# A two-layer hybrid decoder with eight experts: expert results written to DRAM and fetched back per token, in place of scatter products

## The chip, the cores and the metric

The kernel runs on one core of one Trainium2 chip. The metric is the device time of one execution in microseconds (us), the median of several runs. TensorE is called PE, VectorE DVE, ScalarE ACT, GpSimd POOL and SyncE SP.

## The reference

The input x is 256 tokens of 1024 float32. Layer 0 is a state-space mixer beside block attention, then a dense SwiGLU; layer 1 is a linear recurrence beside sparse attention, then a mixture of experts; a final RMSNorm follows. The change touches only how the results of the experts come back to the tokens:

```
logits = xt @ router                      # 256 tokens x 8 experts
top_val, top_exp = top_k(logits, 2)       # two experts per token
gates = softmax(top_val)
...
for each expert e, for its tokens:        # xb: the token rows of e
    yb = (silu(xb @ w_gate[e]) * (xb @ w_up[e])) @ w_down[e]    # 1024 -> 3584 -> 1024
y[token] += yb * gate                     # two contributions per token
h = h + y
out = rms_norm(h, final_norm)
```

## The kernel before

Every engine has a program of its own, written out in order, and they meet at named semaphores. The experts are worked off as *items*. An item is up to 96 tokens (`CAP`) of one expert; items 0 to 7 are the first 96 tokens of experts 0 to 7, and further items exist only when an expert has more than 96 tokens. `n_items` is read from `work_list`, which the routing on DVE fills.

An item has 21 *blocks* (`NEB`), each a weight tile of 2 MiB: 7 of gate, 7 of up, 7 of down. The hidden width 3584 goes in four chunks c = 0 to 3 (`LAST` is 3, and is half as wide); the order is gate and up of c, then down of c-1. SP loads the blocks into seven ring slots: load j is issued once block j-7 has been used (`block_used`). PE multiplies a block in 48 float32 products at lines 2368 and 2370 (each shows as two in the trace, so 96); the hidden units stay token-major, so DVE multiplies (L1648) and turns them by 32x32 transposes (L1629), and ACT does the silu (L961). The item's result, 96 tokens x 1024, gathers in PSUM banks 4 and 5 over all the down blocks.

How a result comes back to its tokens, `it` being the item that follows it:
- ACT (`y_main`, L941 to L944) and DVE (`y_side`, L1606) copy banks 4 and 5 to the tile Y; DVE splits Y into a rounded part and the rest, Yhi and Ylo (L1612, L1614).
- PE multiplies by a 0/1 matrix that places each slot at its token (`scatter`, L2356 and L2357, four products of 512 columns for each half of the tokens), the first half after the second gate block of item `it`, the second half after its first up block.
- DVE adds the placed rows, times their gate, to `htok` (`add_scattered`, L1594).
- That 0/1 matrix is `mine`, made by DVE in chunk 1 of each item, turned (`turn_mine`, L1621), and copied by ACT (L967).

The tokens of the next items are gathered by products as well (`gather`, L2347, 32 products), after the up block of the last chunk of items 0, 2, 4 (for two items at once), 6 and 7. After the last item the same scatter and addition stand at the end, then the final norm and the store. POOL does nothing in this part.

## Time and profile before

| | us |
|---|---|
| median of 3 runs | 1593.23 |
| lowest and highest | 1591.78, 1594.74 |
| time of the profiled execution | 1591.04 |
| its span, first to last instruction | 1589.1 |
| PE busy | 1491.6 |
| DVE busy | 648.5 |
| ACT busy | 277.2 |
| POOL busy | 19.0 |

The span is what the profile covers; 1.94 us of the profiled execution's time lie around it. The experts' part runs from about 657 us to the end. "Busy" of an engine counts its own instructions; whether its time matters is told by who waits for it.

### The profile page before, as it was taken

What the parts mean: (1) busy time and instruction counts of PE and PEld (TensorE: products, weight loads), DVE (VectorE), ACT (ScalarE), POOL (GpSimd) and SP (SyncE); (2) the same over time, 40 slices, a digit from 0 to 9 for tenths busy, and PEclk for the clock granted to TensorE, in tenths of its full rate; (3) what the DMA queues carried; (4) which work ended last, traced back from release to release, by engine and by line L of the source; (5) the groups of instructions that cost most, each with busy time, mean ns of one, the idle gap of its engine ahead of it and who ended that gap; (6) DMA issues with size and microseconds to landing.
All of it is one profiled execution on the core that took longest, in us unless ns stands there. A gap on an engine that the chain in (4) does not pass through costs nothing.

```text
span 1589.1 us, 46789 instructions
## 1 busy us (share of the span) xinstructions
PE 1491.6 (94%) x21833; PEld 1418.5 (89%) x21833; DVE 648.5 (41%) x1486; ACT 277.2 (17%) x472; POOL 19.0 (1%) x21
## 2 busy tenths in 40 slices
PE   7898999997946889899999999999999999999997
PEld 6667999997934778899999999999999999999996
DVE  6933554447477641342142222322333223323323
ACT  3324443434234201200100000000001000001001
POOL 0000000000000210000000000000000000000000
PEclk9999999999966999799999999999999999999998
DMA  9131554463400008399999999999999999999980
GB/s 317 40 131 54 212 212 169 151 223 116 159 1 0 3 15 319 113 390 401 366 370 405 392 385 383 371 394 405 379 394 383 363 399 406 376 401 382 363 333 29
DMA packets 135653, 425.24 MB, mean 268 GB/s; under 512 B 9786, under 2 KB 12964, under 8 KB 135332
## 3 DMA queue, kind: packets, MB, share of 16 engines
q1 hardware_dynamic: 133536, 420.59, 69.6%
q8 instruction: 173, 2.83, 0.7%
q10 hardware_dynamic: 1924, 1.64, 0.4%
q14 instruction: 20, 0.16, 0.0%
HBM read 421.18 MB, written 1.05 MB: 266 GB/s over the span
## 4 chain that ended last, share of the span: by engine, by line
PE 87%; DVE 10%; ACT 2%; issue 1%; DMA 0%; SPq 0%; DVEq 0%; ACTq 0%
PE bank L2370 36%; PE bank L2368 19%; PE bank L1992 5%; PE bank L1994 5%; PE bank L1993 5%; PE bank L1967 2%; PE bank L1736 1%; PE bank L2347 1%; PE bank L1980 1%; PE bank L1902 1%; PE bank L1985 1%; DVE xnT L1008 1%; PE bank L2356 1%; PE bank L2200 1%; PE bank L2185 1%
## 5 line engine op out<-in xcount | busy, mean ns | idle before, releaser
L2370 PE MATMUL bank<-ring,yT 128*32 128x128 f32 x5760 | 635.5, 273 | 0.0
L2368 PE MATMUL bank<-ring,yT 128*32 128x384 f32 x5760 | 631.3, 489 | 1.1 <-ACT yT L934 1.1
L2370 PEld LDWEIGHTS bank<-ring,yT 128*32 128x32 f32 x5760 | 627.6, 110 | 0.0
L2370 PE MATMUL bank<-ring,arena 128*32 128x128 f32 x2304 | 255.6, 273 | 0.0
L2368 PE MATMUL bank<-ring,arena 128*32 128x384 f32 x2304 | 255.1, 490 | 0.0
L2370 PEld LDWEIGHTS bank<-ring,arena 128*32 128x32 f32 x2304 | 251.1, 110 | 0.0
L1994 PE MATMUL bank<-arena_r,ring_r 128*128 128x256 f32 x688 | 193.8, 282 | 0.0
L1629 DVE STREAM_TRANSPOSE arena<-arena 32x192 f32<-32x192 f32 x384 | 142.0, 370 | 124.5 <-PE bank L2370 119.4
L2368 PEld LDWEIGHTS bank<-ring,yT 128*32 128x32 f32 x5760 | 182.0, 108 | 6.4 <-issue 5.1
L1648 DVE TENSOR_TENSOR arena<-arena,bank 128x384 f32<-128x384 f32 x56 | 28.9, 551 | 310.4 <-PE bank L2370 285.9
L1992 PE MATMUL bank<-arena_r,ring_r 128*128 128x256 f32 x528 | 147.9, 280 | 1.3 <-DVE arena_r L1249 1.3
L1993 PE MATMUL bank<-arena_r,ring_r 128*128 128x256 f32 x528 | 147.2, 279 | 0.0
L961 ACT ACTIVATE arena<-bank 128x384 f32<-128x384 f32 x56 | 24.9, 489 | 694.7 <-PE bank L2370 694.7
L1236 DVE TENSOR_TENSOR ring_r<-ring,ring_r 128x2048 fp32r<-128x2048 f32 (+1 forms) x46 | 98.7, 2152 | 89.5 <-ACT ring_r L729 89.4
L1994 PEld LDWEIGHTS bank<-arena_r,ring_r 128*128 128x128 f32 x688 | 130.8, 190 | 0.0
L1992 PEld LDWEIGHTS bank<-arena_r,ring_r 128*128 128x128 f32 x528 | 99.2, 188 | 1.7 <-issue 1.4
L729 ACT ACTIVATE ring_r<-ring 128x2048 fp32r<-128x2048 f32 (+1 forms) x46 | 82.7, 1802 | 95.0 <-PE bank L1994 89.3
L1993 PEld LDWEIGHTS bank<-arena_r,ring_r 128*128 128x128 f32 x528 | 99.1, 188 | 0.1
L2368 PEld LDWEIGHTS bank<-ring,arena 128*32 128x32 f32 x2304 | 65.0, 108 | 0.4
L1594 DVE SCALAR_TENSOR_TENSOR arena<-bank,arena 128x512 f32<-128x512 f32 x32 | 22.5, 746 | 97.2 <-PE bank L2357 97.2
L1992 PE MATMUL bank<-yT_r,ring_r 128*128 128x256 f32 x160 | 46.8, 293 | 8.9 <-DVE arena_r L1242 5.5
L1736 PE MATMUL bank<-xnT,ring 128*128 128x256 f32 x192 | 45.6, 398 | 8.0 <-DVE arena L1206 5.7
(450 smaller groups left out, 1364.7 us busy)
## 6 DMA issues: line engine op xcount, KB each, us to landing
ring<-in_moe_w_gate SPq DMA_DIRECT2D x56, 2048.0 KB, 10.6
ring<-in_moe_w_up SPq DMA_DIRECT2D x56, 2048.0 KB, 10.7
ring<-in_moe_w_down SPq DMA_DIRECT2D x56, 2048.0 KB, 10.7
ring<-in_ffn_w_gate SPq DMA_DIRECT2D x5, 2048.0 KB, 8.1
ring<-in_ffn_w_up SPq DMA_DIRECT2D x5, 2048.0 KB, 7.8
ring<-in_ffn_w_down SPq DMA_DIRECT2D x5, 2048.0 KB, 7.8
ring<-in_o_w_in SPq DMA_DIRECT2D x5, 2048.0 KB, 7.9
ring<-in_e_w_in SPq DMA_DIRECT2D x4, 2048.0 KB, 16.6
```

The lines of the kernel that those rows point to most:

```text
L729: act_.activation(pair(h, src.shape[1])[0], src, ACT.Copy).then_inc(sem("hi_done"), 1)
L961: last = act_.activation(MO["silu"][:, FM * i:FM * i + FM], bank[i][:, 0:FM], ACT.Silu)
L1236: v.tensor_tensor(lo, src, hi.bitcast(f32), SUB).then_inc(sem("lo_done"), 1)
L1629: last = v.transpose(to[QUAD[b], :, 32 * a:32 * a + 32], Hc[QUAD[a], 0:to.shape[1], 32 * b:32 * b + 32])
L1648: last = v.tensor_tensor(MO["H"][:, s_], MO["silu"][:, s_], bank[2 + i][:, 0:FM], MUL)
L1736: last = pe_.matmul(dst(i)[0:width, :], w[:, k, i * P:i * P + width], xnT[:, k, :], start=(k == 0), stop=(k == KD - 1))
L1967: last = pe_.matmul(half(bank[2 + i // 2], i), view(n + i // 4)[:, k, (i % 4) * P:(i % 4) * P + P], yT[:, k, :], start=(k == 0), stop=(k = ...
L1992: pe_.matmul(dst, w[0], x[0], start=start, stop=False, skip_group_check=True)
L1993: pe_.matmul(dst, w[1], x[0], start=False, stop=False, skip_group_check=True)
L1994: return pe_.matmul(dst, w[0], x[1], start=False, stop=stop, skip_group_check=True)
L2368: pe_.matmul(b[QUAD[m], 0:FM], x(m), w[:, 0:FM], start=start, stop=stop, skip_group_check=True)
L2370: last = pe_.matmul(b[QUAD[3], P * m:P * m + P], x(m), w[:, FM:FB], start=start and m == 0, stop=stop, skip_group_check=True)
```

## The change

The results of items 0 to 6 are no longer placed by products. Each is copied to Y as before and then stored by ACT, as 96 rows of 1024 float32 (393,216 bytes), in a DRAM tensor `expert_rows` (`y_store`). In item 0 DVE works out for each token, from its rank in each expert, which two rows are its own (`find_rows`, 18 small operations). When the result of item 6 is stored, POOL issues four indirect transfers, each of 128 rows of 4 KB, into the space of `xnT` and `hT` (2 MiB in all), and in the last chunk of item 7 DVE adds the fetched rows, times their gates, to `htok` (`add_rows`, four operations of 128x1024). A result of expert 7, or of an item beyond 7, is still placed by the products. ACT and DVE write items 0 to 7 out; a loop for items from 8 on follows, which a branch skips if there are none. Before, item 7 was the loop's first turn. Semaphores that the left-out products would have raised are raised in advance.

```diff
+    rows_dram = nc.dram_tensor("expert_rows", ((NE - 1) * CAP, D), f32, kind="Internal").ap()
+    row_of = sb("row_of", NT * 2, i32)
+    rows_in = [flat(x)[:, i * D:i * D + D] for x in (xnT, hT) for i in range(2)]
+    def scattered_by_products(it):
+        return not isinstance(it, int) or it >= NE - 1
...
# POOL
+        pool.wait_ge(sem("mlo_rows_ready"), 2)
+        pool.wait_ge(sem("x_in_Y_out"), 16 * NE)
+        for j in range(NT * 2):
+            pl.indirect_dma_start(rows_in[j], None, rows_dram, bass.IndirectOffsetOnAxis(ap=row_of[:, j:j + 1], axis=0)
+                                  ).then_inc(sem("rows_loaded"), 16)
...
# ACT
+        def y_store(n):
+            act.wait_ge(sem("Y_copied"), 2 * n + 1)
+            act.wait_ge(sem("Y_side"), n)
+            act.dma_start(rows_dram[(n - 1) * CAP:n * CAP, :], MO["Y"][0:CAP, :]).then_inc(sem("x_in_Y_out"), 16)
         def y_main(n):
+            if not isinstance(n, int):
+                act.wait_ge(sem("x_in_Y_out"), 16 * NE)
+            elif n > 1:
+                act.wait_ge(sem("x_in_Y_out"), 16 * n)
...
-            act.wait_ge(sem("mineT_done"), it + 1)
-            act_.activation(mineT[0:CAP, :], mineT0[0:CAP, :], ACT.Copy).then_inc(sem("mineT_copied"), 1)
+            if scattered_by_products(it):
+                act.wait_ge(sem("mineT_done"), it + 1)
+                act_.activation(mineT[0:CAP, :], mineT0[0:CAP, :], ACT.Copy).then_inc(sem("mineT_copied"), 1)
...
-        for it in range(1, NE - 1):
+        for it in range(1, NE):
             run_item(it)
         n_items = act.value_load(work_list[0:1, ITEMS:ITEMS + 1], min_val=NE, max_val=ITEMS)
-        with act.Fori(NE - 1, n_items) as it:
-            run_item(it)
+        with act.If(n_items > NE):
+            with act.Fori(NE, n_items) as it:
+                run_item(it)
...
# DVE, whose loop over the items is changed in the same way
         def y_side(n):
...
             last.then_inc(sem("Y_side"), 1)
+            if isinstance(n, int):
+                return
...
+        def add_rows():
+            dve.wait_ge(sem("rows_loaded"), 16 * NT * 2)
+            for i in range(2):
+                for t in range(NT):
+                    last = v.scalar_tensor_tensor(htok[:, t, :], rows_in[2 * t + i], row_gate[:, t, i:i + 1],
+                                                  htok[:, t, :], MUL, ADD)
...
-            if not peeled:
+            if not isinstance(it, int):
                 for t in range(NT):
                     dve.wait_ge(sem("scatter_done"), NT * it + t + 1)
                     add_scattered(t, 6, sem("scattered"))
...
+                    if peeled:
+                        find_rows()
...
+                if kind == "gate" and c == LAST and isinstance(it, int) and it == NE - 1:
+                    add_rows()
...
# PE
+                if kind == "down" and c == 0 and x == 0 and not peeled:
+                    pe.wait_ge(sem("Y_copied"), 2 * it + 1)
+                    pe.wait_ge(sem("Y_side"), it)
...
-                if kind == "gate" and c == 0 and x == 1 and not peeled:
+                if kind == "gate" and c == 0 and x == 1 and not isinstance(it, int):
                     pe.wait_ge(sem("Yhi_ready"), 2 * it + 1)
                     pe.wait_ge(sem("Ylo_ready"), NT * it)
                     pe.wait_ge(sem("mineT_copied"), it)
                     pe.wait_ge(sem("scattered"), NT * it)
                     scatter(0)
-                if kind == "up" and c == 0 and x == 0 and not peeled:
+                if kind == "up" and c == 0 and x == 0 and not isinstance(it, int):
                     pe.wait_ge(sem("scattered"), NT * it + 1)
                     scatter(1)
```

On PE, at the end of the second gate block of item 1, before the change (`bank` is PSUM, `ring` a weight slot, `yT` the gathered tokens, `arena_r` the placing matrix and the split result):

```order
2988 L2368 MATMUL bank<-ring,yT 32x384 x3
2989 L2370 MATMUL bank<-ring,yT 32x128 x3
2990 L2356 MATMUL bank<-arena_r 128x512 [waits mineT_copied,scattered,Ylo_ready,Yhi_ready]
2991 L2357 MATMUL bank<-arena_r 128x512
2992 L2356 MATMUL bank<-arena_r 128x512
2993 L2357 MATMUL bank<-arena_r 128x512
2994 L2368 MATMUL bank<-ring,yT 32x384 [waits slot1_loaded,H_done]
```

After the change PE has at the same place of item 1:

```order
2986 L2444 MATMUL bank<-ring,yT 32x384 x3
2987 L2446 MATMUL bank<-ring,yT 32x128 x3
2988 L2444 MATMUL bank<-ring,yT 32x384 x3
2989 L2446 MATMUL bank<-ring,yT 32x128 x3
2990 L2444 MATMUL bank<-ring,yT 32x384 [waits slot1_loaded,H_done]
2991 L2444 MATMUL bank<-ring,yT 32x384 x2
```

The four products and the wait for four semaphores are gone, and the gate block is followed at once by the up block; the same holds after the first up block.

On DVE, at the start of item 1, before (L1606 copies a part of Y, L1594 adds the placed rows):

```order
594 L1606 COPY arena<-bank 32x128 [waits block_used]
595 L1606 COPY arena<-bank 32x128 x2
596 L1612 TENSOR_SCALAR arena_r<-arena 96x512 [waits Y_copied,Y_side]
597 L1614 TENSOR_TENSOR arena_r<-arena,arena_r 96x512 [waits Yhi_ready]
598 L1612 TENSOR_SCALAR arena_r<-arena 96x512 [waits Y_copied]
599 L1614 TENSOR_TENSOR arena_r<-arena,arena_r 96x512 [waits Yhi_ready]
600 L1594 SCALAR_TENSOR_TENSOR arena<-bank,arena 128x512 [waits scatter_done]
601 L1594 SCALAR_TENSOR_TENSOR arena<-bank,arena 128x512
602 L1594 SCALAR_TENSOR_TENSOR arena<-bank,arena 128x512 [waits scatter_done]
603 L1594 SCALAR_TENSOR_TENSOR arena<-bank,arena 128x512
604 L1648 TENSOR_TENSOR arena<-arena,bank 128x384 [waits HT_done,block_used,moe_silu]
```

And on DVE in the last chunk of item 7 after the change (`xnT` and `hT` hold the fetched rows):

```order
730 L1667 STREAM_TRANSPOSE arena<-arena 32x6x32 [waits H_done,block_used]
731 L1667 STREAM_TRANSPOSE arena<-arena 32x6x32 x15
732 L1698 SCALAR_TENSOR_TENSOR arena<-xnT,arena 128x1024 [waits rows_loaded]
733 L1698 SCALAR_TENSOR_TENSOR arena<-hT,arena 128x1024
734 L1698 SCALAR_TENSOR_TENSOR arena<-xnT,arena 128x1024 [waits dve_chain]
735 L1698 SCALAR_TENSOR_TENSOR arena<-hT,arena 128x1024
736 L1718 TENSOR_TENSOR arena<-arena,bank 128x384 [waits HT_done,block_used,moe_silu]
737 L1667 STREAM_TRANSPOSE yT<-arena 32x3x32 [waits H_done]
```

The eight operations from L1612 to L1594 leave the start of items 1 to 7, and the four additions stand once, ahead of the last multiplication of item 7.

On ACT, at the start of item 1 after the change:

```order
290 L965 ACTIVATE arena<-bank 96x384 [waits block_used]
291 L966 ACTIVATE arena<-bank 96x384
292 L968 ACTIVATE arena<-bank 32x128 x3
293 L956 DMA expert_rows<-arena 96x1024 [waits Y_side,Y_copied]
294 L987 ACTIVATE arena<-bank 128x384 [waits H_done,block_used]
```

The store is new there; the row after it, the silu, stood directly behind the copies before.

## Rows read from the trace of the kernel before

**Rows 1.** The page: span; PE's busy time; granted clock in 40 slices.
```profile
span 1589.1 us, 46789 instructions
PE 1491.6 (94%) x21833; PEld 1418.5 (89%) x21833; DVE 648.5 (41%) x1486; ACT 277.2 (17%) x472; POOL 19.0 (1%) x21
...
PEclk9999999999966999799999999999999999999998
```

**Rows 2.** Waits of PE from 620 us on: total, times, longest.
```profile
PE bank L2356 <- DVE arena_r L1614: 3.4, 1, 3.4
...
PE bank L2368 <- ACT yT L934: 1.1, 1, 1.1
```

**Rows 3.** Timeline of PE around a scatter in item 2: start, us, instruction.
```profile
893.29 0.82 PE L2370 MATMUL bank<-ring,yT 128*32 128x128 f32 x6
894.04 0.50 PE L2356 MATMUL bank<-arena_r 96*128 96x512 f32 x1
...
894.84 0.40 PE L2357 MATMUL bank<-arena_r 96*128 96x512 f32 x1
895.16 0.52 PE L2368 MATMUL bank<-ring,yT 128*32 128x384 f32 x3
```

**Rows 4.** Timeline of SP's issues of weight loads, without and across scatters.
```profile
662.41 0.37 SPq L497 DMA_DIRECT2D ring<-in_moe_w_up  x1
...
746.25 5.61 SPq L497 DMA_DIRECT2D ring<-in_moe_w_up  x2
...
781.58 7.02 SPq L497 DMA_DIRECT2D ring<-in_moe_w_down  x2
...
894.14 7.02 SPq L497 DMA_DIRECT2D ring<-in_moe_w_down  x2
```

**Rows 5.** Groups by line from 620 us on: the scatter's products.
```profile
L2356 PE MATMUL bank<-arena_r 96*128 96x512 f32 x32 | 15.1, 472 | 3.4 <-DVE arena_r L1614 3.4
```

**Rows 6.** Timeline of PE at the gather of item 2.
```profile
980.40 3.82 PE L2347 MATMUL bank<-arena_r 128*128 128x192 f32 x32
984.15 0.52 PE L2368 MATMUL bank<-ring,arena 128*32 128x384 f32 x3
```

**Rows 7.** Busy time by stretch; last three: granted clock, DMA share, GB/s.
```profile
669.00:782.00 113.00, 113.00 (x2026) 112.46 (x2018) 32.74 (x98) 6.26 (x17) 0.00 (x0) 1.00 1.00 388
...
1270.00:1350.00 80.00, 80.00 (x1473) 80.00 (x1465) 25.07 (x76) 3.35 (x9) 0.00 (x0) 1.00 1.03 402
```

**Rows 8.** Line 497: issue to landing at 662, from 678 to 756, from 660 to 1450.
```profile
DMA to landing us min/median/max: 7.7/7.7/7.7
...
DMA to landing us min/median/max: 10.2/10.9/11.2
...
DMA to landing us min/median/max: 7.6/10.7/12.0
```

**Rows 9.** Timeline of DVE in item 0, chunk 1: turning the hidden units.
```profile
709.58 6.12 DVE L1629 STREAM_TRANSPOSE arena<-arena 32x192 f32<-32x192 f32 x16 [5.19 <-PE bank L2370]
```

**Rows 10.** Groups of DVE at the routing, 630 to 656 us: one small operation.
```profile
L1525 DVE TENSOR_TENSOR arena<-arena 128x16 f32<-128x16 f32 x2 | 0.4, 176 | 0.1
```

**Rows 11.** Timeline of ACT after the copies of Y, item 2.
```profile
894.15 0.87 ACT L961 ACTIVATE arena<-bank 128x384 f32<-128x384 f32 x2 [8.77 <-PE bank L2370]
```

**Rows 12.** Timeline of DVE in the last chunk of item 7, to the end.
```profile
1544.46 6.12 DVE L1629 STREAM_TRANSPOSE arena<-arena 32x192 f32<-32x192 f32 x16 [9.46 <-PE bank L2370]
1554.94 0.55 DVE L1648 TENSOR_TENSOR arena<-arena,bank 128x384 f32<-128x384 f32 x1 [4.36 <-PE bank L2370]
...
1574.51 0.91 DVE L1606 COPY arena<-bank 32x128 f32<-32x128 f32 x3 [14.46 <-PE bank L2370]
```

**Rows 13.** Groups by line from 620 us on: an operation of 128x1024 on DVE.
```profile
L1681 DVE SCALAR_TENSOR_TENSOR arena<-arena 128x1024 f32<-128x1024 f32 x2 | 2.6, 1285 | 0.1
```

**Rows 14.** DMA issues: KB each, us to landing.
```profile
out_dram<-arena SPq DMA_DIRECT2D x2, 512.0 KB, 2.6
...
ring<-in_s_b_re SPq DMA_DIRECT2D x2, 64.0 KB, 5.2
```

More of the change, by code:

```diff
@@ L954, in run_item @@
                 y_main(it)
+                if isinstance(it, int):
+                    y_store(it)
             for j, (kind, c, x) in enumerate(expert_blocks):
@@ L1631, in turn_hidden, with find_rows @@
             last.then_inc(sem("HT_done"), 1)
+        row1, row_gate = (MO["cnt"][:, x:x + NT * 2].rearrange("p (t i) -> p t i", t=NT) for x in (0, NT * 2))
+        def find_rows():
+            wide = [P, NT, NE]
+            link(v.tensor_scalar(flat(e1), flat(rank), 0.0, None, ALU.is_ge))
+            link(v.scalar_tensor_tensor(flat(e1), flat(rank), float(CAP), flat(e1), ALU.is_lt, MUL))
+            link(v.memset(e1[:, :, NE - 1:NE].rearrange("p t o -> p (t o)"), 0.0))
+            link(v.tensor_scalar(e2[:, 0, :], C("expert"), float(CAP), 1.0, MUL, ADD))
+            link(v.tensor_tensor(t16, rank, e2[:, 0:1, :].to_broadcast(wide), ADD))
+            link(v.tensor_tensor(flat(t16), flat(t16), flat(e1), MUL))
+            link(v.tensor_reduce(row1[:, :, 0], t16, AX, ALU.max))
+            link(v.tensor_reduce(row1[:, :, 1], t16, AX, ADD))
+            link(v.tensor_tensor(row1[:, :, 1], row1[:, :, 1], row1[:, :, 0], SUB))
+            link(v.tensor_tensor(flat(e1), flat(e1), flat(gate), MUL))
+            for i in range(2):
+                link(v.tensor_tensor(e2, t16, row1[:, :, i:i + 1].to_broadcast(wide), ALU.is_equal))
+                link(v.tensor_tensor(flat(e2), flat(e2), flat(e1), MUL))
+                link(v.tensor_reduce(row_gate[:, :, i], e2, AX, ADD))
+            link(v.tensor_scalar(flat(row1), flat(row1), -1.0, 0.0, ADD, ALU.max))
+            v.tensor_copy(row_of[:, :], flat(row1)).then_inc(sem("mlo_rows_ready"), 1)
+        def add_rows():
+            dve.wait_ge(sem("rows_loaded"), 16 * NT * 2)
+            for i in range(2):
+                for t in range(NT):
+                    last = v.scalar_tensor_tensor(htok[:, t, :], rows_in[2 * t + i], row_gate[:, t, i:i + 1],
+                                                  htok[:, t, :], MUL, ADD)
+                if not i:
+                    link(last)
         def run_item(it, peeled=False):
@@ L1652, in run_item @@
                         onehots(it + 1, next_items(it))
-                    for t in range(NT):
-                        v.tensor_copy(MO["gnow"][:, t:t + 1], gatep[:, t, bass.ds(it, 1)])
-                    for t in range(NT):
-                        last = v.tensor_scalar(mine[:, t, :], C("time")[:, 0:CAP], slotp[:, t, bass.ds(it, 1)], None,
-                                               ALU.is_equal)
-                    last.then_inc(sem("mine_ready"), 1)
-                    dve.wait_ge(sem("mine_ready"), it + 1)
-                    turn_mine()
+                    if peeled:
+                        find_rows()
+                    if scattered_by_products(it):
+                        for t in range(NT):
+                            v.tensor_copy(MO["gnow"][:, t:t + 1], gatep[:, t, bass.ds(it, 1)])
+                        for t in range(NT):
+                            last = v.tensor_scalar(mine[:, t, :], C("time")[:, 0:CAP], slotp[:, t, bass.ds(it, 1)],
+                                                   None, ALU.is_equal)
+                        last.then_inc(sem("mine_ready"), 1)
+                        dve.wait_ge(sem("mine_ready"), it + 1)
+                        turn_mine()
+                if kind == "gate" and c == LAST and isinstance(it, int) and it == NE - 1:
+                    add_rows()
                 if kind == "up" and x == halves(c) - 1:
@@ L1667, in _ @@
         run_item(0, peeled=True)
-        for it in range(1, NE - 1):
+        for it in range(1, NE):
             run_item(it)
         n_items = dve.value_load(work_list[0:1, ITEMS:ITEMS + 1], min_val=NE, max_val=ITEMS)
-        with dve.Fori(NE - 1, n_items) as it:
-            run_item(it)
+        with dve.If(n_items > NE):
+            with dve.Fori(NE, n_items) as it:
+                run_item(it)
         y_side(n_items)
```

37 lines of the change are left out of this document (23 added, 14 removed).

## The prediction

> **What bounds the kernel now.** I read the page first. PE is busy in 1491.6 of 1589.1 us, and nearly all slices but those of the middle stand at the high clock [rows 1]. A busy PE could still be a slow one that is fed late, so the next view is its list of waits. From 620 us to the end PE waits at most 3.4 us in one place (L2356 at the very end, for Ylo) and 1.1 us in another [rows 2]. Through eight items it waits neither for a weight nor for DVE or ACT. PE's own instructions therefore set the time there, and an instruction taken from it shortens the kernel unless another engine cannot follow.
>
> PE's pace is best read from SP, which issues a load each time PE has used up a block. From 662.41 to 746.25 us there are 16 such steps without any scatter between them: 83.84 / 16 = 5.24 us for a block [rows 4]. From 781.58 to 894.14 us are the 21 steps of item 1 with its two scatters: 112.56 us [rows 4]. The granted clock was 1.00, the 2.4 GHz level, in the stretches read [rows 7]. Twenty-one blocks alone would be 110.04 us, so the two scatters cost 2.52 us in an item, 1.26 us each. The timeline of one agrees: its four products begin at 894.04 and the next block begins at 895.16 us, 1.12 us later [rows 3]; the remaining 0.14 us is PE draining and filling again on both sides.
>
> The other engine to watch is the DMA. Its share is 1.00 to 1.03 in the items, at 388 to 402 GB/s [rows 7], so it looks as full as PE. That share does not say which of them waits. The time to landing does: a lone load of 2 MiB lands after 7.7 us, loads in the steady stretch after 10.2 to 11.2 us, and none between 660 and 1450 us after more than 12.0 us [rows 8]. A load is issued when its slot is freed and is needed six blocks later, 6 x 5.24 = 31.4 us. So at the median of 10.7 us there are 20.7 us of slack.
>
> **The change part by part.**
>
> *Scatter products off PE.* L2356 has 32 instructions, four to an item, so exactly eight items run and none is of a second turn [rows 5]. The scatters of items 0 to 6, which stand inside items 1 to 7, go; that of item 7, at the end, stays. Seven items x 2.52 us = **17.6 us less**. All of it lies on the path, because PE had no idle time around them [rows 2, 3].
>
> *New waits on PE.* At its first down block of an item PE now waits for the copies to Y. These are made at the item's start, and the block is eight blocks or 42 us later, so it is passed at once. Queued behind it would be all of PE; price nothing.
>
> *Y stores on ACT.* ACT now waits for its own and DVE's copies and issues a transfer. What is queued behind is the silu, for which PE waits in turn; but ACT idles 8.77 us before it [rows 11], and an issue takes 0.37 us on SP's queue [rows 4]. The copies of the next item wait for a store made 110 us earlier. A store of 512 KB landed in 2.6 us on a free queue [rows 14], and some 12 us in the full one is the same bound as for a weight. Price nothing on ACT.
>
> *find_rows on DVE, item 0.* Eighteen operations of some 0.18 us [rows 10], with the wait after each about 3.8 us. They stand in chunk 1, where DVE idles 5.19 us before it may turn the hidden units [rows 9], and the operations on `mine` and their turning, which stood in the same gap, leave in that item. Nothing; without that cover 3.8 us once.
>
> *Work that leaves DVE.* Yhi, Ylo and the additions; DVE is not waited for. Nothing.
>
> *add_rows on DVE, item 7.* Four operations of 128x1024, nearest row 1.285 us [rows 13]: 5.1 us. DVE ends its transposes at 1544.46 + 6.12 = 1550.6 us and idles 4.36 us until the last up block is through [rows 12]. So the last product of silu and up comes some 0.9 us later. PE meanwhile gathers for 3.75 us [rows 6] and needs that product only for the last quarter, 2.8 us in; the product takes 0.55 us [rows 12], so 1.3 us are left. Nothing; without that cover 0.9 us.
>
> *The end.* ACT and DVE load n_items and branch over the new loop behind item 7 instead of leaving the old one. DVE idles 14.46 us there [rows 12]. Nothing. The last scatter, the addition and the norm are the same.
>
> *DMA.* This is the only follower that may fail. PE will ask for a block every 5.24 us, 2.097 MB / 5.24 = 400 GB/s, with only the gathers (3.75 us) to catch up in. Added are 0.393 MB for a store in each item (1.0 us of DMA time at 388 GB/s) and 2.1 MB of fetched rows at the start of item 7 (5.4 us). From above: the DMA kept 402 GB/s over 80 us [rows 7], and then nothing piles up but the additions, 7 x 1.0 + 5.4 = 12.4 us, less four gathers of 3.75 us. From below: it can do 388 GB/s and no more, the least of the rows. A block then takes 5.41 us; it falls behind by 3.5 us in an item, with the store 4.5; seven items make 31.5, less four gathers 15.0, plus the fetch 5.4: 21.9 us against 20.7 of slack, a wait of 1.2 us at the end. So the price is 0 to 1.2 us, and if the gathers gave nothing back, 16 us. I take 0: between 678 and 756 us, some 15 loads with one gather and no scatter among them, landings stayed within 10.2 to 11.2 us [rows 8], which is what a DMA that can follow looks like.
>
> The Trainium skill (HBM Reference, Specifications) speaks against the change: it gives a core some 358 GB/s as its share of the memory it has in common with its neighbour, and about 425 when it streams alone. By the first figure a block would take 5.86 us, the kernel would be bound by its loads before and after, and the change would lose the extra traffic; which is the first rival at its extreme; the trace's 402 GB/s disagrees. By the second a block takes 4.93 us and nothing piles up.
>
> *Sum.* 1591.04 - 17.6 = 1573.4 us for an execution like the profiled one. That one lies 2.2 us under the median of the runs shown, so the median should be 1593.23 - 17.6 = **1575.6 us**.
>
> **The rivals.**
> - *The DMA falls behind* and PE waits for weights in items 5 to 7. For it: a share of 1.00, and more bytes in less time. Against it: the slack of 20.7 us and rows 8. The time: 1577 (the wait of 1.2 us) to 1592 (no catching up at all), the middle 1581. Chance 0.11.
> - *The fetch comes late: slower.* The indirect transfers are the one kind that the trace doesn't have. If they went in small pieces as the 64 KB of s_b_re did, which took 5.2 us to land [rows 14], 2048 KB would take 32 x 5.2 = 166 us. They start once item 6's result is stored, near 1470 us in the old times, and DVE wants them at 1550.6: 80 us. They would be 86 us late; DVE stands, the last product is missing, PE stands: 1575.6 + 84 = 1660 us. It turns into a loss when the fetch takes over 80 + 1.3 + 17.6 = 99 us, 21 GB/s. Against it: a fetched row is 4 KB in one piece. Chance 0.04.
> - *A few us given back at the edges:* the start of POOL's first transfers, or the branch at the end. The Trainium skill (Runtime: NRT & Kernel Launch, Instruction fetch mechanics) says that a taken branch out of the two loaded pages has to fetch before it goes on. In rows: such a stall on DVE or ACT has 14.46 us of cover [rows 12], and one of over that would show as a longer wait of PE at the end; 1577 to 1580. Chance 0.07.
> - *Nothing is saved because the products still run:* only with an item beyond 7, which rows 5 rule out for these inputs. Chance 0.
>
> **How the numbers follow.** The forecast has chance 0.78, with a range of its own of 1573 to 1578 (the runs before spread by 3 us). Reaching into the first and third rival, the range 1571 to 1583 holds 0.88 or so by these chances, and I keep that reach, since the cost of the DMA is the least known. A measurement of this kernel tells some 0.2%, 3.2 us, from no change. Faster by more than that: the forecast, the edges and most of the DMA rival, 0.94. Within: the worst of the DMA rival, 0.02. Slower: 0.04.
>
> **What would show it.** In the changed kernel an odd item should last 110.0 us by SP's steps and a block still 5.24; PE's list of waits should stay near what it is. L2356's heir should have 4 instructions. Times to landing may climb to some 16 or 20 us; PE waiting on a weight slot, with landings above 31 us, would be the first rival. A gap of DVE before the four additions would be the second. The prediction is wrong if blocks themselves become slower than 5.24 us, which no row gives a reason for.

## The result, and the profile after

The changed kernel takes 1581.49 us, the median of 4 runs (1581.04 to 1585.56), beside 1593.8 us for the kernel before: a ratio of 0.993, interval 0.9917 to 0.9942. In a second set of runs it took 1579.07 us (5 runs) against 1593.91 us, ratio 0.991 (0.9897 to 0.9923). So it is faster by 12 to 15 us where 17.6 us were forecast. The execution that was profiled first is the slowest of its four, 1585.56 us, and what stands below of it shows more loss than a middle one has.

The page of the changed kernel, answering to [rows 1]:

```profile
span 1583.6 us, 46515 instructions
...
PE 1487.0 (94%) x21777; PEld 1419.3 (90%) x21777; DVE 598.6 (38%) x1340; ACT 275.0 (17%) x465; POOL 22.9 (1%) x25
...
PEclk9999999998975999699999999999999999999998
```

DVE has lost 50 us of work and PE only 4.6 us of busy time, though 56 products went and seven times 2.52 us should be gone. Two single executions don't settle that: PE was busy for 1499.1 us in the second profile of the kernel before (before_again, below) and for 1476.9 us in the second one of the changed kernel. Where time was given back has to be read stage by stage.

The group of the scatter's products by line, the heir of [rows 5], and the timeline of PE at two gathers (start, us, instruction):

```profile
L2432 PE MATMUL bank<-arena_r 96*128 96x512 f32 x4 | 2.6, 662 | 3.4 <-DVE arena_r L1652 3.4
```

```profile
759.87 3.82 PE L2423 MATMUL bank<-arena_r 128*128 128x192 f32 x32
...
983.83 3.81 PE L2423 MATMUL bank<-arena_r 128*128 128x192 f32 x32
```

Four products are left of 32. From gather to gather are two items: 983.83 - 759.87 = 223.96 us. SP's issues, answering to [rows 4], have 21 blocks in 900.09 - 790.05 = 110.04 us, where the kernel before took 112.56 us:

```profile
790.05 5.76 SPq L505 DMA_DIRECT2D ring<-in_moe_w_down  x2
...
900.09 5.76 SPq L505 DMA_DIRECT2D ring<-in_moe_w_down  x2
...
1463.57 7.75 SPq L505 DMA_DIRECT2D ring<-in_moe_w_down  x2
```

The saving of 2.52 us in an item is there to the last digit. The third row is the odd one: its two issues span 7.75 us instead of 5.6, so one block of item 7 took 2.1 us too long.

What PE waits for, from 620 us on (total, times, longest), answering to [rows 2]:

```profile
PE bank L2432 <- DVE arena_r L1652: 3.4, 1, 3.4
...
PE bank L2408 <- DVE arena_r L1619: 0.7, 1, 0.7
PE bank L2446 <- issue: 0.4, 1, 0.4
```

No weight is in the list. Two rows matter. The gather of item 0 (L2408) waits 0.7 us, where it waited 0.36 us; and there is an "issue" row, time in which PE waited for nothing that the profile shows. Time from issue to landing of the weight loads (L505) from 678 to 756, from 780 to 1450 and from 1450 us on, answering to [rows 8]:

```profile
DMA to landing us min/median/max: 9.2/11.0/11.8
...
DMA to landing us min/median/max: 8.6/12.1/15.1
...
DMA to landing us min/median/max: 11.5/15.4/17.8
```

The landings climb, to 17.8 us at most, and 31.4 us would be needed before PE stands. The new transfers by queue, from the page, and by issue (median us to landing), from the view of the DMA:

```profile
q0 software_dynamic: 576, 2.10, 0.3%
...
xnT<-expert_rows,row_of POOLq DMA_INDIRECT x2, 10.1
hT<-expert_rows,row_of POOLq DMA_INDIRECT x2, 12.9
```

The 2.1 MB of rows land 10 to 13 us after their issue near 1465 us, and the additions begin at 1545 us.

PE at the gather of item 0, up to the first block of the experts. First the kernel before, then the changed one:

```profile
651.76 4.02 PE L2332 MATMUL bank<-arena_r,arena 128*128 128x96 f32 x32 [0.36 <-DVE arena_r L1587]
...
656.93 0.52 PE L2368 MATMUL bank<-ring,yT 128*32 128x384 f32 x3 [1.15 <-ACT yT L934]
```

```profile
657.13 7.13 PE L2408 MATMUL bank<-arena_r,arena 128*128 128x96 f32 x32 [0.67 <-DVE arena_r L1619]
665.41 0.52 PE L2444 MATMUL bank<-ring,yT 128*32 128x384 f32 x3 [1.15 <-ACT yT L948]
```

The same 32 products take 7.13 us instead of 4.02 us, and the first block comes 8.28 us after the gather's start instead of 5.17 us. The wait comes from DVE, which is itself idle ahead of the one-hot tile, 0.25 us before the change and 0.54 us after it:

```profile
651.26 0.45 DVE L1587 TENSOR_SCALAR arena_r<-con,arena 128x96 fp32r<-128x96 f32 x2 [0.25 <-DVE arena L1578]
```

```profile
656.63 0.45 DVE L1619 TENSOR_SCALAR arena_r<-con,arena 128x96 fp32r<-128x96 f32 x2 [0.54 <-DVE arena L1607]
```

In the program two semaphore increments stand at this place before the change and five after it. Busy time by stretch shows why (the last three columns are granted clock, DMA share and GB/s); the changed kernel at the first gather, ahead of the gather of item 7, right behind it, and in POOL's burst:

```profile
657.00:665.00 8.00, 7.13 (x32) 6.90 (x32) 0.07 (x1) 0.64 (x3) 0.00 (x0) 0.55 0.00 0
1400.00:1430.00 30.00, 30.00 (x556) 30.00 (x552) 6.93 (x18) 1.36 (x3) 0.00 (x0) 1.00 1.03 405
1436.00:1442.00 6.00, 6.00 (x89) 5.58 (x85) 0.99 (x4) 0.57 (x3) 0.00 (x0) 0.75 0.85 335
1465.00:1469.00 4.00, 3.57 (x45) 1.82 (x44) 0.00 (x0) 0.00 (x0) 2.44 (x3) 1.00 1.03 418
```

Near 0.5 is the 1.2 GHz level: in the first stretch PE ran nearly all of the gather on it, where the kernel before had 0.90 over the same work:

```profile
651.00:657.00 6.00, 4.49 (x37) 3.93 (x40) 0.46 (x3) 1.12 (x5) 0.00 (x0) 0.90 0.00 0
```

In the third, behind the gather of item 7, it is at 0.75, so half of 6 us at the low level. In the fourth the clock is full, and PE's loads have done 44 instructions in 4 us, where a block has 96 of each kind in 5.24 us. Those are three losses, and each got experiments.

### The profile page after: what moved, and what is told of

The parts are those of the page before. It is cut to its first block, busy times and chain, and to the rows that moved or that the text cites. A ratio compares the mean times of both kernels' runs of the same rounds, so it can differ in the third digit from the quotient of the medians.

```text
span 1583.6 us, 46515 instructions
## 1 busy us (share of the span) xinstructions
PE 1487.0 (94%) x21777; PEld 1419.3 (90%) x21777; DVE 598.6 (38%) x1340; ACT 275.0 (17%) x465; POOL 22.9 (1%) x25
## 4 chain that ended last, share of the span: by engine, by line
PE 87%; DVE 9%; ACT 2%; issue 1%; DMA 0%; SPq 0%; DVEq 0%; ACTq 0%
PE bank L2446 37%; PE bank L2444 19%; PE bank L2068 5%; PE bank L2070 5%; PE bank L2069 5%; PE bank L1812 2%; PE bank L2043 2%; PE bank L2423 1%; PE bank L2056 1%; PE bank L1978 1%; PE bank L2061 1%; DVE xnT L1037 1%; PE bank L2276 1%; PE bank L2274 1%; PE bank L2261 0%
## 5 line engine op out<-in xcount | busy, mean ns | idle before, releaser
L2446 PEld LDWEIGHTS bank<-ring,yT 128*32 128x32 f32 x5760 | 628.5, 110 | 1.7 <-issue 1.7
L2444 PEld LDWEIGHTS bank<-ring,yT 128*32 128x32 f32 x5760 | 155.9, 108 | 1.9 <-ACT yT L948 1.4
L1812 PEld LDWEIGHTS bank<-xnT,ring 128*128 128x128 f32 x192 | 39.2, 207 | 15.3 <-DVE arena L1235 5.8
```

Source lines behind the costliest of these rows:

```text
L1812: last = pe_.matmul(dst(i)[0:width, :], w[:, k, i * P:i * P + width], xnT[:, k, :], start=(k == 0), stop=(k == KD - 1))
L2444: pe_.matmul(b[QUAD[m], 0:FM], x(m), w[:, 0:FM], start=start, stop=stop, skip_group_check=True)
L2446: last = pe_.matmul(b[QUAD[3], P * m:P * m + P], x(m), w[:, FM:FB], start=start and m == 0, stop=stop, skip_group_check=True)
```

## The experiments

The kernel before ran beside each of the three later sets of runs, at 1593.91, 1593.73 and 1594.07 us, 11 runs each time. The ratios are to these, and in the first row to 1593.8 us (4 runs).

| kernel | median us (runs) | ratio, interval | gather start to first block | behind item 7's gather | gap in POOL's burst |
|---|---|---|---|---|---|
| changed, first | 1581.49 (4) | 0.993, 0.9917-0.9942 | 8.28 | low clock | yes |
| changed_again | 1579.07 (5) | 0.991, 0.9897-0.9923 | 8.26 | low clock | no |
| no_fetch | 1578.5 (6) | 0.9913, 0.9897-0.9929 | 6.85 | full | none issued |
| direct_fetch | 1577.83 (4) | 0.9899, 0.9885-0.9913 | 4.96 | low clock | none issued |
| no_return_path | 1579.7 (5) | 0.9912, 0.99-0.9925 | 6.69 | full | none issued |
| wide_gather | 1580.85 (6) | 0.992, 0.9906-0.9934 | 6.82 | full | yes |
| late_fetch | 1582.26 (6) | 0.9929, 0.9916-0.9943 | 8.24 | low clock | yes |
| stores_x4 | 1580.57 (5) | 0.9917, 0.9903-0.9931 | 8.25 | low clock | yes |
| fetch_twice | 1580.75 (6) | 0.9924, 0.9908-0.9939 | 6.83 | full | no |
| direct_twice | 1579.97 (6) | 0.992, 0.9898-0.9941 | 8.26 | low clock | none issued |
| sems_later | 1577.52 (4) | 0.9899, 0.9884-0.9913 | 5.26 | low clock | no |
| combined | 1575.14 (4) | 0.9885, 0.9871-0.99 | 5.26 | full | no |

The last three columns are read from the one profiled execution of each, in the timeline of PE. The two profiles of the kernel before have 5.17 and 5.17 us, and full clock.

The columns hold a tie that no experiment was made for. All five profiles with 8.2 or 8.3 us ahead of the first block have the low clock behind item 7's gather. None of the four with 6.7 to 6.9 us has it, and three of these gather 96 columns there like the first five. Of the three with 5.0 to 5.3 us, the two narrow ones have it and the wide one hasn't. Between the first block and that gather PE takes the same 766.4 us in every one of the twelve. So whether the clock falls there seems to hang on when it rose at the start of the experts, and the first two losses aren't independent; why, no run here shows.

**The changed kernel and the kernel before, again.** No edit. One profile each can't tell a property of a kernel from one of an execution.

> The changed kernel once more, nothing edited. In its first profile the experts began at 665.4 us (656.9 before the change) and the last item lost 3.7 us: 2.0 us in a gap of PE inside a block while POOL issued the fetch, and some 1.9 us at the low clock right after the gather at 1431.8. Theory A: the 2.0 us belong to the fetch and come back at the same place; the low clock after the gather and the late start of the experts belong to the single execution. Then the experts' stretch (from the first block to the last scatter) is 905 us, the experts begin within 3 us of 657, and the time is 1578 to 1582. Theory B: both belong to the change (more bytes, a longer start): the experts begin some 8 us late again and the low clock is there again; the time is near 1585.

> The kernel before, once more, for its profile. Its first profile came from the fastest of its runs (1591.0 against a median of 1593.9 us) and its experts began at 656.9 us. In five profiles of the changed kernel and its variants they began at 660.0 to 665.4 us, and the low clock before them lasted longer. Theory A: the stretch ahead of the experts differs from execution to execution in both kernels, and the first profile was a lucky one: they begin at 659 to 665 us now. Theory B: the changed kernel itself loses 3 us and more there: they begin within 1 us of 656.9. In both the experts' stretch should be 920.9 us, unless the clock falls after a gather.

The profile of changed_again shows the late clock at the first gather and the low clock behind item 7's, but no gap in POOL's burst: PE stood in one execution and not in the other, with POOL's transfers at the same place in the program. before_again took 1596.52 us in its one run. Its experts' stretch, first block to last scatter, is 921.2 us beside 920.9 us in the first profile, but the gather of item 0 begins at 657.01 us, not 651.76 us:

```profile
657.01 4.02 PE L2332 MATMUL bank<-arena_r,arena 128*128 128x96 f32 x32 [0.39 <-DVE arena_r L1587]
```

So the stretch ahead of the experts, which the change doesn't touch but for its setting up, differs by 5 us between two executions of one kernel. At 650 us the first profile of the changed kernel was 5.1 us behind the first of the kernel before, and changed_again 0.3 us ahead of it. What differs between the kernels must be read inside the experts' stretch: 920.9 and 921.2 us before, 906.9 and 904.9 us after, where 17.6 us less would be 903.3.

**Without the fetch and the additions.** POOL issues nothing, DVE adds nothing; experts 0 to 6 are missing from the result.

```diff
-        for j in range(NT * 2):
-            pl.indirect_dma_start(rows_in[j], None, rows_dram, bass.IndirectOffsetOnAxis(ap=row_of[:, j:j + 1], axis=0)
-                                  ).then_inc(sem("rows_loaded"), 16)
...
-                    add_rows()
```

> The changed kernel without POOL's four indirect transfers and without the four additions of the fetched rows (the results of experts 0 to 6 are missing in the output); the stores stay. If the fetch makes PE's gap in the last item, the gap is gone and the time falls by 2.0 us against the changed kernel. If the gap comes from something else in the last item (the unrolled code of DVE and ACT, the waits on the stores), it stays and the time is that of the changed kernel within 0.5 us. Times to landing in the last item should not jump from 14 to 18 us.

Measured 1578.5 us beside 1579.07 us for changed_again on the same chip: no difference that can be measured. Item 7, from its first block to the next gather, takes 110.18 us, with no loss in it:

```profile
1430.92 0.52 PE L2437 MATMUL bank<-ring,arena 128*32 128x384 f32 x3
...
1541.10 3.77 PE L2416 MATMUL bank<-arena_r 128*128 128x96 f32 x32
```

The fetch and the additions together are therefore worth little at the median, and the missing 3 us or so must come from elsewhere too.

**The rows fetched by plain transfers on ACT's queue.** The same bytes at the same time, but in row order, so that DVE adds rows that aren't the token's own.

```diff
+                    if c == 0 and isinstance(it, int) and it == NE - 1:
+                        act.wait_ge(sem("x_in_Y_out"), 16 * NE)
+                        for r in range(NT * 2):
+                            act.dma_start(rows_in[r], rows_dram[P * r:P * r + P, :]).then_inc(sem("rows_loaded"), 16)
```

> The changed kernel with the 2 MiB read by four plain transfers from ACT's queue, 128 rows in order, in place of POOL's indirect ones (so the rows added to a token are not its own), issued after the first silu of item 7, at nearly the same time. If it is the bytes that take PE's instructions or weights away, PE has the same gap of about 2 us. If it is POOL's making of the descriptors, the gap is gone and the time is that of no_fetch, 2.0 us less than the changed kernel, while the times to landing jump as before.

1577.83 us. Its profile has no gap in item 7 and happens to have the shortest first gather of those that keep the setting up as it is (4.96 us), but the low clock behind item 7's gather. The bytes themselves cost nothing that shows.

**Without the whole return path.** No fetch, no stores of Y, no waits for them, no indices; experts 0 to 6 are missing.

```diff
-                if isinstance(it, int):
-                    y_store(it)
...
-                    if peeled:
-                        find_rows()
```

> The changed kernel without stores, without the search for rows, without fetch and additions (the results of experts 0 to 6 are missing in the output): only the products are gone. This is the value of the 56 scatter products alone. By the prediction it is 17.6 us under the kernel before. If the stores cost nothing, it equals no_fetch within 0.5 us; if they slow PE or the loads, it lies lower, at most 7 us. The longest time to landing should stay near 13 us instead of climbing to 15.

1579.7 us, no faster than the changed kernel. The stores, the waits that came with them and `find_rows` cost nothing that shows, as they were priced; and even with all of this added work gone 14 us are saved, not 17.6. The increments ahead of the first gather are still in this kernel. What is missing is in what the change does to PE's timing, not in the work that it adds.

**A gather of 192 columns behind item 6.** The changed kernel gathers 96 columns there, for item 7 alone; this one gathers for a pair, and half of it goes unused.

```diff
-            return 1
+            return 2
```

> The changed kernel with the gathers behind items 6 and 7 made for two items, as those behind items 0, 2 and 4 are: 192 columns in each of the 32 products in place of 96. In three of five profiles of variants the granted clock fell to 1.2 GHz right at the end of the gather behind item 6, which cost 1.9 us, and never after the wide ones. If the narrow products matter, the fall is gone, PE's time for the gather stays at 3.7 us, and item 7 takes 110.2 us; the median falls by up to 1.9 us. If the fall has to do with the place alone, it comes after this gather too.

The clock stays at its full level behind the gather, in this profile and in that of combined, which has the same edit. A stretch of combined, with the first block behind the gather starting at 1428.06 us in its middle:

```profile
1425.00:1431.00 6.00, 6.00 (x86) 5.90 (x87) 4.34 (x17) 1.64 (x4) 0.00 (x0) 1.00 1.03 410
```

But wide_gather's median is 1580.85 us; the fall by up to 1.9 us that was expected didn't come. Its profiled execution had the gap in POOL's burst, so its item 7 took 112.10 us. The low clock came in 7 of 10 profiles of changed variants with the narrow gather, in neither of the two with the wide one, and in neither of the kernel before, whose gather there is narrow as well. Two against three of ten is no proof, and wide_gather itself is one of the four profiles with 6.7 to 6.9 us, whose narrow ones had the full clock too. Only sems_later and combined, alike at 5.26 us, speak for the width, so that it matters stays open. What it costs is read: item 7 takes 111.84 us with it (changed_again, sems_later) and 110.18 us without, 1.7 us.

**The fetch late.** POOL also waits until item 7's last seven weight loads have landed, and the additions move behind the last turning of the hidden units.

```diff
+        for j in range(NEB - SLOTS, NEB):
+            pool.wait_ge(*expert_place(NE - 1, j)[1:])
```

> The changed kernel with the fetch issued only when the last weight blocks have landed, and the four additions behind the last turning of the hidden units in item 7, while PE works on the last down block. The fetch then shares the DMA with nothing. If the 2.0 us gap that PE had in item 7 in one of two profiles comes from the fetch beside the weight loads, it cannot come here, and times to landing in item 7 should not exceed 15 us. If the fetch takes over some 20 us, DVE's additions come late and the end moves: 1 to 5 us slower. Otherwise the time is that of the changed kernel or up to 1 us less.

The gap moved with the fetch. The timeline of POOL and that of PE's loads in this kernel:

```profile
1534.75 1.11 POOL L582 DMA_INDIRECT xnT<-expert_rows,row_of  x1 [951.10 <-DMA ring<-in_moe_w_down]
...
1538.65 0.93 POOL L582 DMA_INDIRECT hT<-expert_rows,row_of  x1 [0.30 <-issue]
```

```profile
1538.24 0.14 PEld L2446 LDWEIGHTS bank<-ring,yT 128*32 128x32 f32 x3 [0.35 <-issue]
1538.97 0.42 PEld L2448 LDWEIGHTS bank<-ring,yT 128*32 128x32 f32 x4 [0.56 <-issue]
1539.71 0.11 PEld L2446 LDWEIGHTS bank<-ring,yT 128*32 128x32 f32 x1 [0.32 <-issue]
1540.42 0.15 PEld L2446 LDWEIGHTS bank<-ring,yT 128*32 128x32 f32 x4 [0.60 <-issue]
```

PE stands in pieces, 1.83 us together, from POOL's third transfer on until 0.8 us after the fourth has ended (1538.65 + 0.93). It runs another part of its program there than in the first profile. With the low clock item 7 took 113.68 us. The last weight had landed by then. The expectation that the gap could not come here failed: it doesn't need a DMA full of weight loads.

**Four times the stores.** Y is stored three more times in each item, 1.2 MB more.

```diff
+            for m in range(3):
+                at = (3 * (n - 1) + m) * CAP
+                act.dma_start(more_rows[at:at + CAP, :], MO["Y"][0:CAP, :]).then_inc(sem("x_in_Y_out"), 16)
```

> The changed kernel with each result stored four times, three of them in a DRAM tensor that nothing reads: 1.18 MB more in each of seven items. The DMA then has 3.0 us more work in an item at its rate of 388 to 400 GB/s, 21 us in all, beside the 4.9 that it gained from the stores and the 15 that the gathers give it to catch up. Theory of the slack: landings climb by 2 to 3 us an item to some 28 to 33 us, near the 31.4 us at which PE would wait; the time stays within 1 us of the changed kernel or grows by a few us in item 7. Rival, the DMA is already the bound: PE waits for weights from item 2 or 3 on and the time grows by about 20 us.

1580.57 us, the same as without. Landings of its weight loads up to 1450 us, and from there on:

```profile
DMA to landing us min/median/max: 7.6/18.4/27.2
...
DMA to landing us min/median/max: 18.8/24.9/30.9
```

They climb to 30.9 us, just under the 31.4 us at which PE would stand, and its list of waits has no weight in it. The slack worked out before is real, and the change uses at most 17.8 - 10.7 = 7.1 of its 20.7 us.

**The fetch twice, by POOL or by ACT.** The second four transfers start when the first have landed; by ACT the rows are again not the token's own.

```diff
+        for m in range(2):
+          if m:
+            pool.wait_ge(sem("rows_loaded"), 16 * NT * 2)
+          for j in range(NT * 2):
...
-            dve.wait_ge(sem("rows_loaded"), 16 * NT * 2)
+            dve.wait_ge(sem("rows_loaded"), 16 * NT * 4)
```

> The changed kernel with POOL's four transfers issued a second time once the first four have landed (the same rows again). In four of five profiles with POOL's transfers PE had a gap of about 2.0 us inside a block while POOL issued them, wherever in item 7 they stood; in none of the three without them. If POOL's transfers make the gap, there are now two gaps, some 10 to 15 us apart, and item 7 takes up to 2 us more than with one. If the gap is chance, there is one or none.

> The same bytes twice, but by plain transfers from ACT's queue as in direct_fetch (the rows added are not the token's own). If the bytes alone made the gap, PE has two gaps here too, 4 us in all. If it is the way POOL issues, there is none, and the time is that of direct_fetch, 1578 us.

If a burst of POOL's stopped PE each time, fetch_twice would have two gaps. It has none, although POOL issued twice (first row of either burst):

```profile
1456.58 1.11 POOL L583 DMA_INDIRECT xnT<-expert_rows,row_of  x1 [870.40 <-DMA expert_rows<-arena]
...
1473.91 0.94 POOL L583 DMA_INDIRECT xnT<-expert_rows,row_of  x1 [12.49 <-DMA hT<-expert_rows,row_of]
```

Item 7 of fetch_twice takes 110.18 us, so 4.2 MB of rows in place of 2.1 are free as well. direct_twice has no gap either and loses only the low clock's time. The medians, 1580.75 and 1579.97 us, don't tell them apart. The theory that each burst stops PE fell: the burst makes the gap possible, not certain.

**DVE's advance increments later.** The changed kernel sets five semaphores ahead, once, to their final counts before the one-hot tile of item 0, for which PE waits. Two of these were there before. Here all five stand behind it.

```diff
-        dve.sem_inc(sem("scattered"), NT * NE)
-        dve.sem_inc(sem("Yhi_ready"), 1 + 2 * (NE - 1))
-        dve.sem_inc(sem("Ylo_ready"), NT * (NE - 1))
-        dve.sem_inc(sem("mine_ready"), NE - 1)
-        dve.sem_inc(sem("mineT_done"), NE - 1)
```

> The changed kernel with DVE's advance semaphore increments (three more than before, ahead of the one-hot matrices that the first gather waits for) moved behind those matrices. PE's first gather began 0.3 us later in the changed kernel than before, and the low clock then lasted 3.4 to 6.8 us into it in six of eight profiles (some 2 to 3 us lost), in neither of two profiles of the kernel before. If that 0.3 us is what does it, the gather starts as before, the experts begin 5.2 us after the gather's start, and the median falls by 2 to 3 us to some 1577. If it is the phase of the clock alone, the gather is still slow in most executions and the median stays at 1579 to 1581.

The timeline of PE in sems_later:

```profile
655.56 4.11 PE L2408 MATMUL bank<-arena_r,arena 128*128 128x96 f32 x32 [0.15 <-DVE arena_r L1614]
660.82 0.52 PE L2444 MATMUL bank<-ring,yT 128*32 128x384 f32 x3 [1.15 <-ACT yT L948]
```

PE idles 0.15 us, not 0.67, and the gather takes 4.11 us, not 7.13. In all ten profiles with the five increments ahead PE idled 0.66 or 0.67 us there; the step from gather to first block took 7.34 us in their mean, 2.2 us more than before. In two without them it took 5.26 us each. So 0.3 us of semaphore instructions go with a loss of about 2.2 us, because the granted clock comes up later. It isn't bound to: direct_fetch, with 0.67 us of idling, took 4.96 us. At the medians, 1577.52 us lies 1.6 and 4.0 us under the two of the changed kernel; its interval overlaps with that of the nearer one. The profile shows the gain more surely than the medians.

**The three together.** The increments later, the wide gather, and POOL's four transfers one by one, a transfer for every three blocks:

```diff
+            pool.wait_ge(sem("block_used"), NEB * (NE - 1) + 2 + 3 * j)
```

> A candidate that is to beat both kernels: sems_later, the wide gathers behind items 6 and 7, and POOL's four transfers apart from each other, one after each third block of item 7. If a burst of transfers is needed to starve PE, the gap is gone (item 7 takes 110.2 us); if each transfer costs PE some 0.5 us, four small gaps of 2 us in all remain. Expected with all three losses gone: 1593.8 - 17.6 = 1576 us; with the gaps 1578.

1575.14 us (1574.41 to 1576.0), ratio 0.9885 (0.9871 to 0.99): 18.9 us under the kernel before and below every one of the nine runs of the changed kernel (1577.03 to 1585.56). Its timelines of PE at the first gather and of POOL:

```profile
652.69 4.11 PE L2409 MATMUL bank<-arena_r,arena 128*128 128x96 f32 x32 [0.15 <-DVE arena_r L1615]
```

```profile
1455.33 1.11 POOL L581 DMA_INDIRECT xnT<-expert_rows,row_of  x1 [870.35 <-PE bank L2447]
1470.46 0.94 POOL L581 DMA_INDIRECT xnT<-expert_rows,row_of  x1 [14.02 <-PE bank L2447]
```

Item 7 takes 110.17 us. This is the forecast's size of gain, reached only when what the change gave back is taken away. How much of it the spacing brings isn't known: the gap is absent from half of the profiles without spacing too.

**The gap itself, looked at closer.** In the first profile of the changed kernel, POOL and PE's loads:

```profile
1463.21 1.11 POOL L580 DMA_INDIRECT xnT<-expert_rows,row_of  x1 [875.87 <-DMA expert_rows<-arena]
...
1465.87 0.94 POOL L580 DMA_INDIRECT hT<-expert_rows,row_of  x1 [0.30 <-issue]
1467.12 0.93 POOL L580 DMA_INDIRECT hT<-expert_rows,row_of  x1 [0.31 <-issue]
```

```profile
1466.68 0.11 PEld L2446 LDWEIGHTS bank<-ring,yT 128*32 128x32 f32 x1 [0.46 <-issue]
...
1467.41 0.12 PEld L2444 LDWEIGHTS bank<-ring,yT 128*32 128x32 f32 x2 [0.42 <-issue]
...
1468.83 0.14 PEld L2446 LDWEIGHTS bank<-ring,yT 128*32 128x32 f32 x2 [1.24 <-issue]
```

Three stops, 2.12 us, inside one block, with nothing for which PE waits. Such a gap of about 2 us stands in 4 of the 8 profiles with POOL's transfers (changed, wide_gather, late_fetch, stores_x4), each time in pieces that end 0.8 us after the burst does, and in none of the 4 without them. With so few profiles the count alone would be weak; that in late_fetch gap and burst both came 77 us later in item 7 is the stronger sign. The transfers by queue in that stretch, 1455 to 1480 us (packets, MB, share), name a candidate:

```profile
q0 software_dynamic: 575, 2.10, 21.2%
...
q8 instruction: 3, 0.05, 0.8%
```

The instruction queue q8 moved three packets of 16 KB here. The Trainium skill (Runtime: NRT & Kernel Launch, Instruction fetch mechanics) says that each engine's sequencer fetches the next page of 256 instructions while it works through the present one, and that crossing a page's end is mostly hidden. By that rule nothing stands. A page that comes late would fit the stop, but the rows don't bear it out. With the low clock's 1.7 us taken off, the stop begins 29.1 us behind item 7's first block both in the first profile and in wide_gather, whose bursts began at 26.1 and 26.0 us. In sems_later the burst begins at 25.8 us, runs over the same place, and there is no stop. So this cause is argued, not shown.

## Why the prediction was right, and where its size was off

**The products, 17.6 us: right.** An odd item takes 110.04 us by SP's steps, against 110.0 foreseen; the block is 5.24 us; two items from gather to gather take 223.96 us; four products are left. All variants show it.

**The DMA, 0 to 1.2 us: right, 0.** Landings climbed to 17.8 us, within the 16 or 20 foreseen, and no weight was waited for. stores_x4 is the stronger witness: with 1.2 MB more in each item they reached 30.9 us and the time stayed. So the first rival had its mechanism right, bytes that pile up, and its point of decision 14 us away. Taking the trace's 402 GB/s over the lower figure of the Trainium skill (HBM Reference, Specifications, some 358 GB/s to a core that shares) held: the changed kernel moved 405 GB/s in 30 us ahead of item 7. That section gives the 358 GB/s for both cores of a pair streaming and about 425 for one alone, and this kernel runs on one core, so it didn't speak against the change as the prediction had it. By an estimate from its 358 GB/s, 5.86 us for a block, PE would have stood for weights everywhere.

**The fetch late: fell.** It lands in 10 to 13 us, not in the 99 us at which it would have lost. Issues of 0.94 to 1.11 us on POOL are what it costs that engine. The row from which that rival was priced, 5.2 us for 64 KB, was no guide to rows of 4 KB.

**Stores, new waits, `find_rows`: right at nothing, as far as medians tell.** no_return_path, which has none of them, isn't faster.

**`add_rows`: right at nothing.** DVE in the last chunk of item 7, answering to [rows 12]:

```profile
1545.07 1.28 DVE L1698 SCALAR_TENSOR_TENSOR arena<-xnT,arena 128x1024 f32<-128x1024 f32 x1
...
1548.79 1.28 DVE L1698 SCALAR_TENSOR_TENSOR arena<-hT,arena 128x1024 f32<-128x1024 f32 x1
1549.99 0.55 DVE L1718 TENSOR_TENSOR arena<-arena,bank 128x384 f32<-128x384 f32 x1
```

The four take 4.9 us until the next operation starts, 1.28 us each as priced by the row of 1.285 us. The product behind them is done at 1550.54 us. PE's gather starts at 1549.30 us and needs it for its last quarter, 2.8 us in, at 1552.1 us, so 1.6 us are to spare where 1.3 us were foreseen. (The prediction's rows, 1550.58 + 5.14 - 1554.94, give 0.8 us of delay, not 0.9; measured against the gather's start it is 0.6 us.) In fetch_twice, without gap, item 7 is 110.18 us all the same.

**The end: no loss, but not quite the same.** The last wait of PE is still 3.4 us. The last eight products start 0.43 us apart, at the low clock, in both profiles of the kernel before and in five of the twelve changed ones; in the other seven most of them start 0.23 us apart, which makes the end 1.3 to 1.4 us shorter. The prediction had no term for that.

**The step that was mis-sized: what the change costs at nothing.** It left out one edit and took PE's clock for a constant. The semaphore increments that DVE now makes ahead of time, three more than before, weren't in the list of edits at all; they stand in front of the one tile for which PE waits at the start of the experts. Measured: 0.3 us later, 2.2 us lost on the mean of ten profiles. The low clock behind item 7's gather came in addition, 1.7 us in 7 of 10, and PE's stop in POOL's burst, 2.0 us in half. For the first the cause is shown by sems_later; for the other two it stays open. Together: -17.6 + 2.2 + 1.7 x 0.7 + 2.0 x 0.5 = -13.2 us; the nine runs of the changed kernel have their median at 1581.04 us, 12.9 us under the kernel before at 1593.9. The shorter end, some 1.4 us in 6 of these ten, would make it -14.0 us; the two sets of runs say 12.3 and 14.8 us less. So the terms cover what is missing to within about 1 us, no closer, and the last ones come from few profiles.

In the terms of the rivals, the third happened on top of the forecast: "a few us given back at the edges", with the start of POOL's transfers named as a place. Its chance, 0.07, was far too low, its own 1577 to 1580 us were exceeded too, and its branch at the end had no part in it. The forecast's own range, 1573 to 1578 us, was missed by 3.5 us. The wide one, 1571 to 1583 us, held the time, but it was kept wide mainly for the cost of the DMA, which was nothing. That it covered losses of another kind was luck.

**The base.** The sum was made against one execution, 1591.04 us, which lay 2.2 us under its median; the second profile of the kernel before shows that such differences arise ahead of the experts, 5 us in 650. Moving the forecast by the median's distance was right.

## What to carry to other kernels

Products taken off a full PE come back at their full step time, 1.26 us here for 1.12 us of visible products, if the other engines have slack; read that slack as time to landing against time to need, not as the DMA's share, which was 1.00 to 1.03 before and after. Then list every instruction that the edit puts ahead of a tile for which PE waits, semaphore increments too, and ask at which clock PE does the next work: behind an idle stretch 0.3 us can cost 2 to 3. And judge a gain of a per cent stage by stage on two profiles of either kernel, since untouched stages differ by 5 us from one execution to the next.

## What the runs showed of the hardware

- A little idling at the wrong place moved the granted clock: at the first gather 0.90 before and 0.55 after, for 0.3 us more of idling, though one of ten such profiles had it up in time. And it fell to the 1.2 GHz level behind a gather in the middle of gapless work, at 1.7 us each, in 7 of 10 profiles of changed variants with 96 columns; by the table that went with how late it had risen at the first gather.
- While POOL issued indirect transfers PE could stand for about 2.0 us though it waited for none of them: 4 of 8 profiles, and none of 4 without them. Twice as many transfers gave no gap in the one profile taken. The cause is open; runs that place the burst at set distances from PE's instruction transfers would tell.
- Indirect loads of 128 rows of 4 KB cost POOL 0.94 us each (1.11 the first) and landed in 10.1 to 12.9 us in a DMA that was moving 400 GB/s; the same bytes by plain loads from ACT's queue (direct_fetch) took 9.6 to 14.3 us.
- The DMA's share was 1.03 from 1400 to 1430 us in both kernels, with a median of 11.3 us to landing before and 14.6 us after: the share doesn't tell how near it is to holding PE up.
